# A decoder trunk step: pieces of the conditioning product moved out of the gate and down loops, and tables loaded by another queue

## The reference

```python
silu_c = jax.nn.silu(c)                       # c: one row per sequence, 9 rows
...
mod = (silu_c @ p['w_ada'][l] + p['b_ada'][l]).reshape(B, N_MOD, D)
m = [mod[:, j][:, None, :] for j in range(N_MOD)]
hh = modulate(rmsnorm(x, p['g_pre'][l, 0]), m[0], m[1])
f = swiglu(hh, p['w_ffn_gate'][l, 0], p['w_ffn_up'][l, 0], p['w_ffn_down'][l, 0])
x = x + 0.5 * m[2] * rmsnorm(f, p['g_post'][l, 0])
```

## Time and profile before

| | |
|---|---|
| Median of 3 runs | 1593.86 us (1589.09 to 1594.75) |
| Profiled execution | 1594.14 us, span 1592.5 us |
| Mean granted TensorE clock | 0.929 of 2.4 GHz |
| PE busy | 1420.3 us (89% of the span) |
| DVE, ACT, POOL busy | 795.9, 617.8, 101.9 us |
| DMA | 260.03 MB, 163 GB/s over the span |

### The profile page before, as it was taken

How to read it: one execution, slowest core, us unless ns; L and a number is a source line. 1 busy time by engine, 2 the same in 40 slices (tenths; PEclk the granted TensorE clock), 3 DMA queues, 4 the chain that set the end, 5 groups by cost and what they waited for, 6 DMA issues and landing times.

```text
span 1592.5 us, 24138 instructions
## 1 busy us (share of the span) xinstructions
PE 1420.3 (89%) x9602; PEld 1294.0 (81%) x9602; DVE 795.9 (50%) x1416; ACT 617.8 (39%) x1026; POOL 101.9 (6%) x184
## 2 busy tenths in 40 slices
PE   3899999969889886999999699999969676999995
PEld 1799989959776585999989599998959575999995
DVE  0544443376775547444433644443366777444444
ACT  1533333353322245333333443333345655434332
POOL 0001000022001000101010000000000000000000
PEclk7899999989986787999999899999989887999998
DMA  9567656536231143666566456655343221444342
GB/s 335 211 222 235 219 181 231 171 127 199 83 126 56 44 159 105 235 221 230 197 207 234 145 172 199 204 182 196 128 155 107 82 81 54 158 156 142 113 157 72
DMA packets 80608, 260.03 MB, mean 163 GB/s; under 512 B 10690, under 2 KB 21362, under 8 KB 80386
## 3 DMA queue, kind: packets, MB, share of 16 engines
q1 hardware_dynamic: 58562, 180.17, 34.1%
q0 software_dynamic: 21952, 78.54, 14.9%
HBM read 254.45 MB, written 4.23 MB: 162 GB/s over the span
## 4 chain that ended last, share of the span: by engine, by line
PE 84%; DVE 9%; ACT 3%; DMA 2%; issue 1%; SPq 0%; DVEq 0%; ACTq 0%
PE ps L1328 25%; PE ps L1330 23%; PE ps L1329 23%; PE ps L1359 4%; PE ps L1380 3%; DVE rstd L1702 2%; DVE w_lo L1662 1%; PE ps L686 1%; DMA w_raw<-in_gu 1%; PE ps L609 1%; PE ps L617 1%; ACT w_hi L1498 1%; DVE f L1728 1%; DMA a_raw<-in_ada 1%; PE ps L636 1%
## 5 line engine op out<-in xcount | busy, mean ns | idle before, releaser
L1328 PE MATMUL ps<-xn_hi,w_hi 128*128 128x320 f32 x1872 | 599.9, 320 | 60.8 <-DVE xn_lo L1723 29.7
L1329 PE MATMUL ps<-xn_lo,w_hi 128*128 128x320 f32 x1872 | 586.0, 313 | 0.0
L1330 PE MATMUL ps<-xn_hi,w_lo 128*128 128x320 f32 x1872 | 585.7, 313 | 0.0
L1662 DVE TENSOR_TENSOR w_lo<-w_raw,w_hi 128x1024 fp32r<-128x1024 f32 x362 | 387.4, 1111 | 195.5 <-ACT w_hi L1498 194.6
L1328 PEld LDWEIGHTS ps<-xn_hi,w_hi 128*128 128x128 f32 x1872 | 359.0, 192 | 94.1 <-issue 87.8
L1498 ACT ACTIVATE w_hi<-w_raw 128x1024 fp32r<-128x1024 f32 x362 | 330.2, 961 | 132.4 <-PE ps L1330 112.3
L1329 PEld LDWEIGHTS ps<-xn_lo,w_hi 128*128 128x128 f32 x1872 | 359.3, 192 | 1.3
L1330 PEld LDWEIGHTS ps<-xn_hi,w_lo 128*128 128x128 f32 x1872 | 358.6, 192 | 0.0
L1328 PE MATMUL ps<-mid_hi,w_hi 128*128 128x320 f32 x704 | 220.0, 312 | 2.7 <-DVE mid_lo L1751 2.7
L1330 PE MATMUL ps<-mid_hi,w_lo 128*128 128x320 f32 x704 | 217.4, 309 | 0.0
L1329 PE MATMUL ps<-mid_lo,w_hi 128*128 128x320 f32 x704 | 217.4, 309 | 0.0
(11 more groups left out here) (237 smaller groups left out, 931.4 us busy)
## 6 DMA issues: line engine op xcount, KB each, us to landing
w_raw<-in_gu SPq DMA_DIRECT2D x176, 512.0 KB, 4.8
a_raw<-in_ada POOLq DMA_DIRECT2D x128, 512.0 KB, 4.1
w_raw<-in_down SPq DMA_DIRECT2D x64, 512.0 KB, 3.6
w_raw<-in_pj SPq DMA_DIRECT2D x58, 512.0 KB, 4.6
w_raw<-in_down SPq DMA_DIRECT2D x64, 192.0 KB, 3.6
a_raw<-in_ada SPq DMA_DIRECT2D x16, 512.0 KB, 7.5
cached<-in_pages_kv POOLq DMA_DIRECT2D x16, 192.0 KB, 4.4
st_in<-in_state_ret POOLq DMA_DIRECT2D x4, 512.0 KB, 4.8
```

The lines of the kernel that those rows point to most:

```text
L1328: pe.matmul(out, hi, xhi, start=start, stop=False)
L1329: pe.matmul(out, hi, xlo, start=False, stop=False)
L1330: return pe.matmul(out, w_lo[s][:, w_at:w_at + P], xhi, start=False, stop=stop)
L1662: dve.tensor_tensor(w_lo[s][:, cols], w_raw[:, s, cols], w_hi[s][:, cols].bitcast(F32), ALU.subtract).then_inc(w_split, 1)
```

## The change

The pieces get a new plan. Gate0 keeps 16 (one ahead of each of tiles 0 to 15) and down0 8. The boundaries take 16, 16, 16, 8 and 8: "sum" ahead of the output's sum matmul, "root" behind it, "square" behind the named k of the squares' matmuls, "first" ahead of the named k of the next stage's first tile. The four heads of attention take 8 each, the odd mixer's tail 8. The attention's 32 pieces are loaded by SP into eight places of lent memory, the two slots of w_raw and slot 0 of w_hi and w_lo. `ada_row` has six rows in place of one, so that units 5 to 10 are turned together at the end of attention; the table `ADA_TURNS` says where each unit is turned. The tables of both mixers are loaded by SP, between its second and third weight tile of the stage. The wait for the odd stores goes from the end of `gp_odd` to the end of POOL's queue.

```diff
 ADA_PLAN = [("front", 0, 2 * KC)]
-ADA_PLAN += [("gate0", c, 2 - c % 2) for c in range(FC - 1)]
-ADA_PLAN += [("down0", m, 2) for m in range(KC)]
-ADA_PLAN += [("gate1", c, 2 - c % 2) for c in range(FC - 1)]
-ADA_PLAN += [("down1", m, 2) for m in range(KC)]
-ADA_PLAN += [("gate2", c, 1) for c in range(FC - 2)]
-ADA_PLAN += [("down2", m, 2 if m < 6 else 0) for m in range(KC)]
+ADA_PLAN += [("gate0", c, 1 if c < 2 * KC else 0) for c in range(FC)]
+ADA_PLAN += [("down0", m, 1) for m in range(KC)]
+def into(stage, sums, roots, squares, firsts):
+
+
+    plan = [(stage, "sum", sums), (stage, "root", roots)]
+    plan += [(stage, ("square", k), 1) for k in squares]
+    return plan + [(stage, ("first", k), 1) for k in firsts]
+
+
+ADA_PLAN += into("even_in", 2, 4, (2, 5), range(KC))
+LENT = 8
+ADA_PLAN += [("attention", h, LENT) for h in range(RH)]
+ADA_PLAN += into("gate1", 2, 4, (2, 5), range(KC))
+ADA_PLAN += into("gate2", 2, 4, (2, 5), range(KC))
+ADA_PLAN += into("odd_in", 2, 4, (), (2, 5))
+ADA_PLAN += [("odd_tail", 0, KC)]
+ADA_PLAN += into("gate3", 2, 4, (), (2, 5))
...
-def units_at(stage, i):
-
...
+ADA_TURNS = {("front", 0): [0, 1], ("gate0", 7): [2], ("gate0", 15): [3], ("down0", 7): [4],
+             ("attention", 0): [5, 6, 7, 8, 9, 10],
+             ("gate1", 0): [11], ("gate1", 1): [12], ("gate2", 0): [13], ("gate2", 1): [14],
+             ("odd_out", 0): [15, 16], ("gate3", 0): [17]}
+A_ROWS = 6
...
+A_RANK = {p: r for r, p in enumerate(p for p in range(KC * A_UNITS) if p not in set(pieces_of("attention")))}
+A_HELD = {r: p for p, r in A_RANK.items()}
...
-        def ada_loads(gp, stages):
-
-            for stage, i, _ in ADA_PLAN:
-                if stage in stages:
-                    for p in ADA_PIECES[stage, i]:
-                        gp.wait_ge(a_used, p - A_SLOTS + 1)
-                        gp.dma_start(a_raw[:, p % A_SLOTS, :], row(t["ada"], p)).then_inc(a_landed[p % A_SLOTS], 16)
+        def lent(q):
+
+            cols = slice(1024 * (q % 2), 1024 * (q % 2 + 1))
+            return w_raw[:, q // 2, cols] if q < 4 else (lent_hi, lent_lo)[q // 2 - 2][:, cols]
+
+        def ada_load(gp, pieces):
+
+            for p in pieces:
+                r = A_RANK[p]
+                gp.wait_ge(a_used, A_HELD[r - A_SLOTS] + 1)
+                gp.dma_start(a_raw[:, r % A_SLOTS, :], row(t["ada"], p)).then_inc(a_landed[r % A_SLOTS], 16)
 
         def gp_even(gp):
 
-            gp.wait_ge(w_used, CR + W_BASE["even_in"])
-            gp.dma_start(perm[:, :, :], t["perm"]).then_inc(perm_in, 16)
-            for dst, src in ((bias_p[:, :, :], t["bias_p"]), (bias_s[:, :], t["bias_s"]),
-                             (rep_s[:, :, :], t["rep_s"]), (sel_s[:, :, :], t["sel_s"]),
-                             (hmask[:, :], t["hmask"]), (dec_p[:, :, :], t["dec_p"]),
-                             (qdec[:, :, :], t["qdec"]), (kdec[:, :, :], t["kdec"]),
-                             (bmask[:, :], t["bmask"]), (dec_s[:, :, :], t["dec_s"])):
-                gp.dma_start(dst, src).then_inc(even_in_dma, 16)
-            gp.dma_start(ones_h[:, :], t["ones_h"]).then_inc(perm_in, 16)
             gp.wait_ge(xn_ready, 8 * (PREP["even_in"] + 1))
             gp.dma_start(ropet, t["rope"]).then_inc(rope_in, 16)
...
+        def even_constants(sp_):
+
+            sp_.wait_ge(w_used, CR + W_BASE["even_in"])
+            sp_.dma_start(perm[:, :, :], t["perm"]).then_inc(perm_in, 16)
+            sp_.dma_start(ones_h[:, :], t["ones_h"]).then_inc(perm_in, 16)
+            for dst, src in ((bias_p[:, :, :], t["bias_p"]), (bias_s[:, :], t["bias_s"]),
+                             (rep_s[:, :, :], t["rep_s"]), (sel_s[:, :, :], t["sel_s"]),
+                             (hmask[:, :], t["hmask"]), (dec_p[:, :, :], t["dec_p"]),
+                             (qdec[:, :, :], t["qdec"]), (kdec[:, :, :], t["kdec"]),
+                             (bmask[:, :], t["bmask"]), (dec_s[:, :, :], t["dec_s"])):
+                sp_.dma_start(dst, src).then_inc(even_const, 16)
...
-            pe.wait_ge(mod_ready, units_at("down0", KC - 1)[-1] + 1)
+            pe.wait_ge(mod_ready, 5)
             pe.wait_ge(perm_in, 32)
 
             both_blocks("even_in", base % 2, (0, 1), True).then_inc(w_used, 1)
             for b in range(1, EVEN_BLOCKS):
                 if b > 1:
                     block_of(base + b // 2, b, b % 4, (base + b // 2) % 2, b % 2)
+                if b == 1:
+                    pe.wait_ge(row_ready, 7)
...
                 logits(2 * h + 1)
+                if h:
+                    pe.wait_ge(pv_out, 2 * h)
+                ada_pieces("attention", h)
                 turn(2 * h)
                 inner(h)
+                pe.wait_ge(row_ready, 8 + h)
                 weigh(2 * h)
                 cross(h)
...
             for u in (N_PU, N_PU + 1):
                 turn(u)
                 weigh(u)
-
-        def act_even(act, steps, split_w, n_half):
+            ada_transpose("attention", 0)
+
...
+            ada_copy(5, 6)
...
             for h in range(RH):
                 spread(h)
                 exponents(2 * h)
+                ada_copy(7 + h)
                 act.wait_ge(kv_done, h + 1)
...
             for k in range(KC):
                 low(k)
+            ada_bias("attention", 0)
...
-        def gp_odd(gp):
-            gp.wait_ge(w_used, CR + W_BASE["odd_in"])
+        def odd_constants(sp_):
+            sp_.wait_ge(w_used, CR + W_BASE["odd_in"])
             for dst, src in ((cst[:, :, :, :], t["conv_state"]), (cw[:, :, :], t["conv_w"]), (cb[:, :, :], t["conv_b"]),
                              (brg[:, :, :], t["b_rg"]), (h0[:, :, :], t["h0"]), (wrg[:, :, :], t["w_rg"])):
-                gp.dma_start(dst, src).then_inc(odd_in_dma, 16)
+                sp_.dma_start(dst, src).then_inc(odd_in_dma, 16)
+
+        def gp_odd(gp):
             gp.wait_ge(tails_ready, 1)
             gp.dma_start(t["tails"], tails[:, :, :, :]).then_inc(odd_stored, 16)
             gp.wait_ge(hl_ready, 1)
             gp.dma_start(t["hlast"], hlast[:, :, :]).then_inc(odd_stored, 16)
-            gp.wait_ge(odd_stored, 32)
-
...
+                if c == 2:
+                    pe.wait_ge(row_ready, 16)
                 if c > 1:
                     gates(c - 2)
             gates(KC - 2)
             gates(KC - 1)
-
-        def act_odd(act, steps, split_w, n_half):
+            pe.wait_ge(rg_act, 2 * KC - 3)
+            ada_pieces("odd_tail", 0)
+
...
+            ada_copy(15)
             act.wait_ge(odd_in_dma, 16 * 6)
...
+            def lent_loads():
+
+                pieces = pieces_of("attention")
+                for i, p in enumerate(pieces):
+                    q = i % LENT
+                    if i < 4:
+                        sp_.wait_ge(w_split, CR + 2 * (W_BASE["even_out"] + q // 2))
+                    elif i < LENT:
+                        sp_.wait_ge(w_used, CR + W_BASE["even_out"])
+                    else:
+                        sp_.wait_ge(a_used, p - LENT + 1)
+                    sp_.dma_start(lent(q), row(t["ada"], p)).then_inc(a_lent[q], 16)
+                sp_.wait_ge(a_used, pieces[-1] + 1)
 
             gate_loads(0)
             down_loads(0)
-            proj_loads("even_in", 0, EVEN_IN_TILES)
-            proj_loads("even_out", EVEN_IN_TILES, OUT_TILES)
+            proj_loads("even_in", 0, range(2))
+            even_constants(sp_)
+            proj_loads("even_in", 0, range(2, EVEN_IN_TILES))
+            proj_loads("even_out", EVEN_IN_TILES, range(1))
+            lent_loads()
+            proj_loads("even_out", EVEN_IN_TILES, range(1, OUT_TILES))
             gate_loads(1)
             down_loads(1)
             gate_loads(2)
             down_loads(2)
-            proj_loads("odd_in", EVEN_IN_TILES + OUT_TILES, ODD_IN_TILES)
-            proj_loads("odd_out", EVEN_IN_TILES + OUT_TILES + ODD_IN_TILES, OUT_TILES)
+            proj_loads("odd_in", EVEN_IN_TILES + OUT_TILES, range(2))
+            odd_constants(sp_)
+            proj_loads("odd_in", EVEN_IN_TILES + OUT_TILES, range(2, ODD_IN_TILES))
+            proj_loads("odd_out", EVEN_IN_TILES + OUT_TILES + ODD_IN_TILES, range(OUT_TILES))
...
                 for k in range(KC):
+                    ada_pieces(stage, ("first", k))
                     pe.wait_ge(xn_ready, 8 * PREP[stage] + k + 1)
...
-                for p in ADA_PIECES.get((stage, i), ()):
+                for p in at_pieces(stage, i):
                     u, k = divmod(p, KC)
-                    if k == 0 and u >= 2:
-                        pe.wait_ge(row_ready, u - 1)
                     if p < 2 * KC:
                         pe.wait_ge(a_first[p % A_SLOTS], 16 * (p // A_SLOTS + 1))
+                    elif stage == "attention":
+                        n = p - pieces_of(stage)[0]
+                        pe.wait_ge(a_lent[n % LENT], 16 * (n // LENT + 1))
+                        part = lent(n % LENT)
+                        out, cols = 7, slice(0, ADA_COLS)
```

(72 more changed lines are left out.)

74 lines of the change are left out of this document (38 added, 36 removed).

## The result

| | before | after |
|---|---|---|
| Median, same chip | 1592.01 us (1589.09 to 1594.75, 4 runs) | 1566.13 us (1562.89 to 1568.63, 4 runs) |
| Profiled execution, span | 1594.14, 1592.5 us | 1567.02, 1565.3 us |
| Mean granted clock | 0.929 | 0.937 |
| PE busy | 1420.3 us | 1416.2 us |

The ratio is 0.9833 [0.9808, 0.9859] (95% interval): 1.7% faster, where 1569 us (1.6%) was forecast. Of eleven more runs of the kernel before, seven took 1587.9 to 1591.0 us at a mean clock of 0.933 to 0.936 and four 1594.0 to 1598.9 us at 0.926 to 0.929; the profiled execution (1594.14 us at 0.929) is one of the slower kind. PE does the same work, so its busy time hardly moves. What changed is where that work lies.

The account below looks back on a forecast made before the run. PE's stream was taken to bound the kernel, with 84% of the last-ending chain. From 1594.14 us, 65.3 us removed and 40.2 us added gave 1569.0 us; own range 1557 to 1582, 8 times in 10 1546 to 1588.

Parts of the forecast that it names:

- The loops: Gate and down loops: 104 of 144 pieces move out, saving 63.3 us, and five fewer transposes save 2.0 us.
- "Sum" and "root": Boundaries, around the output's sum matmul: two and four pieces fit in PE's idle gaps and cost nothing.
- Squares: Two pieces inside the squares' matmuls in each of three boundaries: 1.0 us each, 3.0 us in all.
- Odd tail: Eight pieces in the odd mixer's tail, under its 23.4 us with PE nearly idle: cost nothing.
- Firsts: Next stage's first tile: pieces exceed the 0.44 us slack per k; 3.8, 5.3, 4.5 and twice 1.5, 16.6 us.
- Attention: Eight pieces in each of four heads, where PE is nearly never idle: 18.5 us added, ends -2 and 42.
- heads 1, 2 and 3 with the clock that each has now: Attention's heads 1 to 3: eight pieces cost 3.9, 7.7 and 3.9 us at unchanged clocks, 15.5 us.
- second case: Rival: clock rises where pieces fill gaps, attention +3, firsts 8.5, 11.5 us added; 1540 us in full, chance 0.19.
- Head 0: Attention's first head: its pieces' data land at 473.5 us and PE is done at about 474, adding 3.0 us.
- third case: Rival: loads at 207 GB/s set the heads' length, heads 1 and 3 lasting 25 us; 1587 us, chance 0.12.
- Tables on SP: Both mixers' tables, 12 and 6 DMA issues between weight loads on SyncE: cost nothing, bounds -1 and +3 us.
- End of attention: Six transposes at attention's end, where PE idles 3.38 us: 2.1 us added, ends 0 and 3.

Follow-up runs that it names:

- the gap version: Kernel after, boundary pieces moved: six at "root", none in squares, firsts ahead of k = 0, leftover two ahead of k = 4 and 7; 1550.37 us (0.9728).
- the kernel without pieces: Kernel after with attention's 32 pieces, their matmuls and loads left out, row copies and transposes kept; 1564.95 us (0.9832).
- the table run: Kernel after with both mixers' table loads back on POOL, between piece loads; 1568.02 us.
- the filled loops: The gap version with gate and down loop pieces grouped and some set ahead of the waits between gate and down; 1533.20 us (0.9635).
- half-load: Kernel after where head 0 reads its first four lent pieces twice and the other four are not loaded; 1558.80 us.

## Why the prediction was right

The time is 3 us from the forecast, and the steps are these.

The loops: right. 63.3 us for pieces and 2.0 for transposes were forecast to go; gate1 gave 20.1 (forecast 19.8 and a transpose's share), gate2 14.2 (14.6), down2 7.8 (7.3), gate0 with down0 11.1 (11.8 and a transpose's share), down1 8.2 (9.8). With the 1.1 us that two turns together add in odd_out it is 60.3 in place of 65.3. Some of the missing 5 us is the clock: the same 2 us wait for mid_lo was followed by low stretches in down0 and down1 of this trace (some 1.5 us each) and not in the kernel before. The prediction looked at the clock in boundaries and attention only. What makes the clock fall behind this wait in one trace and not in the other stays open, as the two traces of the kernel after differ in it too.

"Sum" and "root": right, nothing. Squares 4.7 us in place of 3.0: within the ends given. About 4 us of it lie in the three boundaries with pieces in the squares (2.0, 1.4 and 0.6 from the squares' start to the next weights); odd_in, which has none there, adds 0.9. Odd tail: nothing, as forecast; the odd mixer and odd_out together are 1.5 us longer, which is the 0.4 of the first tile and the 1.1 of the turns.

Firsts: 16.6 us forecast, 16.6 measured, as 5.3, 4.8 and 4.75 (forecast 3.8, 5.3, 4.5) and 0.4 and 1.3 (1.5 each). The mechanism, a slack of 0.44 us per k that can't take a 0.77 us piece, is seen in the 1.64 us from k to k (forecast 1.65; at the low level 2.9, forecast 3.04), and shown by the gap version, which asks it of two k and not of seven and gets the time back.

Attention: the term that was mis-sized, 18.5 us against 8.5 between the traces and, against the kernel without pieces, 6.8 by traces and 2.4 by medians. The step that failed is "heads 1, 2 and 3 with the clock that each has now": head 2 was taken at its 0.50 and given +7.7, and went -1.8, while heads 1 and 3 went +3.3 and +2.6 for 3.9 each. More than half of the 9.5 us in head 2 is the luck of one trace, since the unaltered kernel is 5.5 us shorter there in its other one. Held against that other trace the four heads grow by 4.4, 3.2, 3.6 and 3.6 us, 14.8 in all, close to the price at the high clock.

That the pieces give time back rests on the runs with the pieces left out and with their matmuls doubled: both say less than half of a fixed price, by 1564.95 against 1567.37 us, and by 6.3 us of heads against 14. That the clock is what gives it back fits, but isn't shown. Time at the low level over the heads is 47.8, 30.8 and 47.8 us in the three traces without pieces, 30.7, 30.7, 34.1, 34.1 and 44.3 us in five with them (the kernel after twice, the table run, the filled loops, the gap version), 17.1 us with the matmuls doubled and 13.6 to 23.8 us in three with other loads for head 0. The first two sets overlap. The prediction's second case, held at 0.19, was right in direction for attention at most (though 8.5 is not its 3) and wrong for the first tiles, whose clocks of 0.81 to 0.83 lie between the two of the earlier trace rows.

Head 0 had the right reason, its loads, at too low a price: +4.4 in place of +3.0. Removing the waits gave 10 us against one trace and 5.8 against another. The error of 10 us in attention was offset by the 5 us that the loops and odd_out fell short, by 1.7 in the squares and by 2.0 in down3 and even_out: the total is closer than its parts deserve.

The Trainium skill (TensorE: Matmul & The Clock Gate, "HAM oscillation — how this bites in real kernels") has a PE that stalls between bursts falling to half rate, and staying at the full one where its work is long against the waits. The half-load and the doubled-matmul runs agree (head 0 at 1.00 in both, 0.69 in the kernel after). The waits alone don't decide, though, as head 0 is at 0.84 in the table run with the same ones. Nor does busy time: PE was busy for 20.49 of 22.40 us in head 1 of the kernel without pieces, at 0.50.

The third case (loads hold every head) fell except for head 0: heads 1 to 3 show no such length, at 195 to 281 GB/s. Tables on SP: nothing, as forecast, and the other way costs 2.7 us in that boundary. End of attention: 1.7 in place of 2.1.

Left open: how the low stretches distribute over the heads. They move between versions in which nothing of attention was edited: in the gap version the heads took 90.3 us, with 1 and 2 at 21.5 and 23.5, and in the table run 86.5 us with the same two lengths. A term of attention below some 6 us can't be read from one trace.

## What to carry to other kernels

Before moving filler work into idle time, read in the timeline exactly ahead of which wait the idle time lies: whole groups ahead of that wait cost nothing as long as their loads have landed, while one piece per step of a pipeline with 0.44 us of slack a step cost 5 us a tile. Where filler stays in a busy stream, group it, since the first piece of a group costs 0.77 us and the next ones 0.44. A stage that sits at the low clock has no fixed price for added matmuls: hold two traces of the same kernel against each other first, before a price is read from either. A wait for a load in front of it can cost more than its own length: the same 4.4 to 4.8 us of waits came with 7.4 us at the low level in one trace and 16.7 in another.
